# Per-head norms, rotary turns and gates computed inside the projections that feed them, and expert outputs written as plain rows

## The reference

```python
# first block, even layer: gated linear attention, its output gated by silu(r)
o = o * lax.rsqrt(jnp.mean(o * o, axis=-1, keepdims=True) + EPS)
o = (o * g_gla * jax.nn.silu(r))
# first block, odd layer: attention, 8 query heads, 2 key/value heads of 128
q = rms_norm((h @ w_q).reshape(B_, L, ATT_HEADS, HEAD_DIM), g_q)   # then apply_rope(q, cos, sin)
k, v = ...                                                          # k: rms_norm, then apply_rope on the latents
def apply_rope(t, cos, sin):
    t1, t2 = jnp.split(t, 2, axis=-1)
    return jnp.concatenate([t1 * cos - t2 * sin, t1 * sin + t2 * cos], axis=-1)
s = jnp.einsum('bkgqd,bksd->bkgqs', q, k) * (HEAD_DIM ** -0.5)      # softmax over s, times v
# second block: HGRN2 gates, forward and backward, from columns q, f_fw, f_bw, i, g of h @ w_in
logf = jnp.log(lbd + (1.0 - lbd) * jax.nn.sigmoid(fr))
kf = (1.0 - lbd) * jax.nn.sigmoid(-fr)          # cumulative sums of logf, exponentials, chunked scan
o = o * lax.rsqrt(mean(o * o) + EPS) * norm_g * jax.nn.silu(g)
# second block: mixture of 64 experts, each of 512 tokens goes to 8
y = _swiglu(h[tok], wg[e], wu[e], wd[e]) * gw[:, None]
out = out.at[tok].add(y)                        # sum over a token's 8 experts, plus a shared expert
```

## Time and profile before

| | |
|---|---|
| time, median of 3 runs | 4281.18 us (4280.32 to 4283.61) |
| the profiled execution's own time | 4279.15 us |
| its span in the profile | 4277.3 us |
| busy: PE, PEld | 3600.4 us (84%), 2155.2 us (50%) |
| busy: DVE, ACT, POOL | 1260.6 us (29%), 832.1 us (19%), 338.0 us (8%) |
| HBM read, written | 454.25 MB, 37.22 MB |
| granted PE clock, mean | 0.907 |

### The profile page before, as it was taken

The page is one execution under the profiler, slowest core; times in us unless marked ns, Lnnn a source line. Parts: engine busy times, 40 slices in busy tenths (PEclk is TensorE's granted clock), DMA queues, the critical chain, the costliest instruction groups (busy, mean ns, idle before and its releaser), DMA issues. The chain is left out here.

```text
span 4277.3 us, 63533 instructions
## 1 busy us (share of the span) xinstructions
PE 3600.4 (84%) x26072; PEld 2155.2 (50%) x26072; DVE 1260.6 (29%) x2655; ACT 832.1 (19%) x1497; POOL 338.0 (8%) x439
## 2 busy tenths in 40 slices
PE   4698568999999977999998948996956879999975
PEld 1255354555555535644443528993525445555543
DVE  0000352222210126322204584444026232222222
ACT  0010331211100113321101052332033212222211
POOL 2000000000000000000001000000000024343332
PEclk7799778999999987999998959997977889999997
DMA  9911001111111100022211000000100369999996
GB/s 385 388 45 41 3 25 40 45 54 50 45 54 46 58 16 25 25 79 79 76 68 68 30 9 3 4 4 33 54 15 27 117 220 342 344 347 347 341 366 221
DMA packets 97371, 485.34 MB, mean 113 GB/s; under 512 B 14912, under 2 KB 19552, under 8 KB 66320
## 3 DMA queue, kind: packets, MB, share of 16 engines
q1 hardware_dynamic: 74352, 435.21, 27.1%
q0 software_dynamic: 22816, 47.14, 4.8%
HBM read 454.25 MB, written 37.22 MB: 115 GB/s over the span
## 5 line engine op out<-in xcount | busy, mean ns | idle before, releaser
L438 PE MATMUL psum<-arena 128*128 128x512 f32 x2112 | 1018.7, 599 | 52.5 <-PEq L1048 29.6
L536 PE MATMUL psum<-arena 128*128 128x512 f32 x1408 | 663.8, 593 | 4.2 <-ACT arena L376 4.2
L438 PEld LDWEIGHTS psum<-arena 128*128 128x128 f32 x2112 | 402.6, 191 | 322.8 <-issue 278.6
L2700 PE MATMUL psum<-arena 128*64 128x256 f32 x3072 | 357.6, 380 | 41.5 <-DMA arena<-exp_w_in 41.3
L440 PEld LDWEIGHTS psum<-arena 128*128 128x128 f32 x1168 | 221.8, 190 | 283.6 <-issue 283.6
L536 PEld LDWEIGHTS psum<-arena 128*128 128x128 f32 x1408 | 266.3, 189 | 194.1 <-issue 172.8
L440 PE MATMUL psum<-arena 128*128 128x256 f32 x1168 | 349.2, 379 | 0.0
L2700 PEld LDWEIGHTS psum<-arena 128*64 128x64 f32 x3072 | 222.0, 135 | 206.5 <-DMA arena<-exp_w_in 60.1
L564 DVE SCALAR_TENSOR_TENSOR arena<-psum,arena 128x511 f32<-128x511 f32 (+1 forms) x132 | 83.2, 658 | 552.2 <-ACT arena L548 552.2
L538 PEld LDWEIGHTS psum<-arena 128*128 128x128 f32 x704 | 133.1, 189 | 169.6 <-issue 169.6
L538 PE MATMUL psum<-arena 128*128 128x256 f32 x704 | 209.7, 378 | 0.0
(11 more groups left out here) (460 smaller groups left out, 4277.1 us busy)
## 6 DMA issues: line engine op xcount, KB each, us to landing
arena<-exp_w_in SPq DMA_DIRECT2D x207, 1024.0 KB
arena<-w_mod_r_in SPq DMA_DIRECT2D x18, 4096.0 KB
arena<-w_ffn_up_in SPq DMA_DIRECT2D x88, 512.0 KB, 3.3
arena<-w_ffn_down_in SPq DMA_DIRECT2D x16, 1408.0 KB, 5.9
arena<-w_in_in SPq DMA_DIRECT2D x35, 512.0 KB, 3.2
arena<-w_even_in_in SPq DMA_DIRECT2D x17, 512.0 KB, 3.3
arena<-w_qkv_in SPq DMA_DIRECT2D x12, 512.0 KB, 3.2
arena<-acc SPq DMA_DIRECT2D x12, 512.0 KB, 8.1
```

The lines of the kernel that those rows point to most:

```text
L438: mm = pe.matmul(ps[:, 2 * b, :], lhsT, src[:, k, 0:LAT], start=(k == 0), stop=(k == kt - 1))
L536: mm = pe.matmul(ps[:, 2 * b, :], lhsT, A[:, k, 0:LAT], start=(k == 0), stop=(k == KD - 1))
L2700: mm = pe.matmul(ps[64 * c:64 * c + 64, 0, 0:256], xt[u][:, k, :], wgu[w][:, k, :, c * P:(c + 1) * P], start=(k == 0), stop=(k == KD - 1))
```

## The change

- `project("qkv")` and `qk_norm_rope` become one stage, `qkv_in`. The weights are rolled, so that the keys come first, then the values, then the queries; the list `QKV_JOBS` orders 12 tiles, two jobs `kn` and two `vt` over three pairs of PSUM banks. ACT squares each tile from PSUM, PE sums the squares over the channels as one column per 128 tokens (44 small matmuls), DVE turns the raw tile from PSUM with three products with the gain (two of them of half height, reading one half of the partitions and writing the other) and a sum. The keys' roots are spread to rows by 12 matmuls with the identity and multiplied in (`kn`); the queries' roots are not multiplied in but handed to attention as a scale per row (`rq`). The permutation and the reciprocals of whole tiles go.
- `project("hgp")` and `hgrn_gates` become `hgrn_in`: the f tiles come first, ACT takes the sigmoids, Silus and copies from PSUM as tiles finish, with the logarithms of one direction after tiles 3 and 7 and the exponentials after tiles 5 and 10; DVE's sums and products run beside them. The copy by POOL becomes a DMA on SP in `hgrn_scan`.
- The gates' Silu in `head_norm` goes: `project("evi")` and `hgrn_in` apply it on the way out of PSUM.
- Experts: each (token, expert) pair has its own row in `yrows` (16 half rows of 2 KB per token). The scatter writes without adding and skips empty slots by a bounds check. The zeroing goes. The routing table has a third value per (token, expert), the pair's rank within the token, made by 4 scans on DVE. At the end SP reads 32 KB per token in four DMAs of 4 MB into two buffers, and the shared expert's 2 MB; DVE folds 8 rows to 4 and 4 to 2, and PE sums the rest with the shared part while it transposes (24 matmuls for each of the four).

The diff, cut to its core:

```diff
-        project(nc, m, "evi", evi, m["A"], [T] * 17, copy_out(m, big, [T] * 17), norm=Norm(m, T, 0, (0, 0)))
+        project(nc, m, "evi", evi, m["A"], [T] * 17, copy_out(m, big, [T] * 17, range(8, 12)), norm=Norm(m, T, 0, (0, 0)))
...
-        sizes = [LAT] * 8 + [T] * 4
-        project(nc, m, "qkv", qkv, m["A"], sizes, copy_out(m, big, sizes), norm=Norm(m, T, 2, (1, 0)))
-        qk_norm_rope(nc, m, io)
+        qkv_in(nc, m, io, qkv, Norm(m, T, 2, (1, 0)))
...
-        sizes = [LAT] * 4 + [T] * 12 + [LAT] * 4
-        project(nc, m, "hgp", hgp, m["A"], sizes, copy_out(m, big, sizes), norm=Norm(m, T, 4, (2, 0), kept=True))
-        hgrn_gates(nc, m, io)
+        hgrn_in(nc, m, hgp, Norm(m, T, 4, (2, 0), kept=True))
...
+        return "act", lambda act, s, b: act.activation(dst[:, t, 0:sizes[t]], pair_banks(m["ps"], b, sizes[t]),
+                                                       ACT.Silu if t in silu else ACT.Copy)
...
-                act.activation(r[:, h, 0:n], r[:, h, 0:n], ACT.Silu).then_inc(s["sr"], 1)
...
+QKV_JOBS = [("k", 0), ("k", 1), ("v", 0), ("v", 1), ("q", 0), ("kn", 0), ("q", 1), ("kn", 1), ("q", 2), ("vt", 0), ("q", 3),
+            ("vt", 1), ("q", 4), ("q", 5), ("q", 6), ("q", 7)]
...
+def qkv_in(nc, m, io, feed, norm):
...
+    released = {"k": ("rope", 0), "q": ("rope", 2), "kn": ("kn", 0), "v": ("vc", 0), "vt": ("vo", 0)}
...
+            def sums(kind, i):
+                n = turned(kind, i)
+                if n == 0:
+                    pe.wait_ge(s["nxn"], KD)
+                pe.wait_ge(s["sq"], n + 1)
+                for t in range(width(kind) // P):
+                    o = ps[:, 6, i * TT + t:i * TT + t + 1] if kind == "k" else ps[:, 7, 4 * i + t:4 * i + t + 1]
+                    mm = pe.matmul(o, sq[:, n % 2, t * P:(t + 1) * P], m["ones"][:, 0:1], start=True, stop=True)
+                mm.then_inc(s["sm"], 1)
+
+            norm.pe(pe, s)
+            f, before = 0, None
+            for j, (kind, i) in enumerate(QKV_JOBS):
+                b = j % 3
+                if j >= 3:
+                    was, w = QKV_JOBS[j - 3]
+                    sem, base = released[was]
+                    pe.wait_ge(s[sem], base + w + 1)
+                if kind == "kn":
+                    pe.wait_ge(s["kr"], 1)
+                    for t in range(TT):
+                        c = i * TT + t
+                        mm = pe.matmul(ps[:, 2 * b + t // 4, t % 4 * P:(t % 4 + 1) * P],
+                                       kroot[:, c:c + 1].to_broadcast([P, P]), m["ident"], start=True, stop=True)
+                    mm.then_inc(s["wide"], 1)
+                elif kind == "vt":
+                    pe.wait_ge(s["vc"], i + 1)
+                    for t in range(TT):
+                        mm = pe.transpose(ps[:, 2 * b + t // 4, t % 4 * P:(t % 4 + 1) * P], dst[:, 10 + i, t * P:(t + 1) * P],
+                                          m["ident"])
+                    mm.then_inc(s["vt"], 1)
+                else:
+                    feed.arrived(pe, f)
+                    for k in range(KD):
+                        if f == 0:
+                            pe.wait_ge(s["na"], k + 1)
+                        lhsT = feed.tile(m, f)[:, k, :]
+                        mm = pe.matmul(ps[:, 2 * b, :], lhsT, m["A"][:, k, 0:LAT], start=(k == 0), stop=(k == KD - 1))
+                        if kind != "q":
+                            mm = pe.matmul(ps[:, 2 * b + 1, 0:CTX], lhsT, m["A"][:, k, LAT:T], start=(k == 0), stop=(k == KD - 1))
+                    mm.then_inc(s["mm"], 1)
+                    f += 1
+                    if before is not None:
+                        sums(*before)
+                    before = (kind, i) if kind != "v" else None
+            sums(*before)
...
+                if kind in "kq":
+                    n, w = turned(kind, i), width(kind)
+                    if n >= 2:
+                        act.wait_ge(s["sm"], n - 1)
+                    act.activation(sq[:, n % 2, 0:w], pair_banks(ps, b, w), ACT.Square).then_inc(s["sq"], 1)
...
+                    if i == 1:
+                        act.wait_ge(s["sm"], 2)
+                        act.activation(kroot, ps[:, 6, 0:12], ACT.Sqrt, scale=1.0 / P, bias=m["misc"][:, 0:1]
+                                       ).then_inc(s["krt"], 1)
...
+                    p, x, t = ps[:, 2 * b, :], dst[:, h, 0:LAT], t1[:, n % 2, :]
+                    g = cols[:, COL["gqk"] + h:COL["gqk"] + h + 1]
+                    dve.wait_ge(s["sq"], n + 1)
+                    if n >= 2:
+                        dve.wait_ge(s["fin"], n - 1)
+                    dve.scalar_tensor_tensor(x, p, g, cos, MUL, MUL)
+                    dve.scalar_tensor_tensor(t[lo, :], p[hi, :], g[hi, :], sin[hi, :], MUL, MUL)
+                    last = dve.scalar_tensor_tensor(t[hi, :], p[lo, :], g[lo, :], sin[lo, :], MUL, MUL)
+                    if kind == "k":
+                        last = dve.tensor_scalar(dst[:, h, LAT:T], ps[:, 2 * b + 1, 0:CTX], g, None, MUL)
+                    last.then_inc(s["rope"], 1)
+                    dve.wait_ge(s["rope"], n + 1)
+                    dve.tensor_tensor(x, x, t, ADD).then_inc(s["fin"], 1)
+                if (kind, i) == ("k", 1):
+                    dve.wait_ge(s["krt"], 1)
+                    dve.reciprocal(kroot, kroot).then_inc(s["kr"], 1)
+                if kind == "kn":
+                    x = dst[:, 8 + i, :]
+                    dve.wait_ge(s["wide"], i + 1)
+                    dve.wait_ge(s["fin"], i + 1)
+                    dve.tensor_tensor(x, x, pair_banks(ps, b, T), MUL).then_inc(s["kn"], 1)
+            dve.wait_ge(s["qrt"], 1)
+            own.link(dve.reciprocal(qroot, qroot))
+            dve.tensor_scalar(rq[:, 0, :], qroot, scale, None, MUL)
+            dve.tensor_scalar(rq[:, 1, :], qroot, -scale, None, MUL)
...
-                dve.tensor_scalar(x[:, 0:1], x[:, 2:3], -scale, None, MUL).then_inc(s["nm"], 1)
+                dve.tensor_tensor(x[:, 0:1], x[:, 2:3], rq[:, 1, g:g + 1], MUL).then_inc(s["nm"], 1)
...
+def hgrn_in(nc, m, feed, norm):
...
+    sizes = [T] * 8 + [LAT] * 4 + [T] * 4 + [LAT] * 4
...
-            pool.tensor_copy(m["A"][:, 0:4, 0:LAT], at(HG_Y, 4, T)[:, :, 0:LAT])
...
+            def logs(d):
+                act.wait_ge(s["act"], 4 * d + 4)
+                for n in range(4 * d, 4 * d + 4):
+                    act.activation(cum[:, n, :], cum[:, n, :], ACT.Ln, scale=lb1[:, n:n + 1], bias=lb[:, n:n + 1]
+                                   ).then_inc(s["ln"], 1)
+
+            def decays(d):
+                for n in range(4 * d, 4 * d + 4):
+                    act.wait_ge(s["mid"], n + 1)
+                    act.activation(q_hat(n), cum[:, n, 0:LAT], ACT.Exp).then_inc(s["ep"], 1)
+                    act.wait_ge(s["ep"], n + 1)
+                    act.activation(cum[:, n, :], cum[:, n, :], ACT.Exp, scale=-1.0).then_inc(s["en"], 1)
+
+            norm.act(act, s)
...
+            for t in range(N):
+                x = pair_banks(ps, t % 4, sizes[t])
+                act.wait_ge(s["mm"], t + 1)
+                if t < 8:
+                    act.activation(cum[:, t, :], x, ACT.Sigmoid)
+                    out = act.activation(f[:, t, :], x, ACT.Sigmoid, scale=-1.0)
+                elif t < 12:
+                    out = act.activation(q[:, t - 8, :], x, ACT.Silu)
+                elif t < 16:
+                    out = act.activation(v[:, t - 12, :], x, ACT.Copy)
+                else:
+                    out = act.activation(g[:, t - 16, :], x, ACT.Silu)
+                out.then_inc(s["act"], 1)
+                if t in (3, 7):
+                    logs(t // 4)
+                if t in (5, 10):
+                    decays(t // 8)
...
+            def sums(d):
+                for n in range(4 * d, 4 * d + 4):
+                    dve.wait_ge(s["ln"], n + 1)
+                    running_sum(dve, m["rst64"], cum[:, n, :], cum[:, n, :], d).then_inc(s["cu"], 1)
+                    if n % 4:
+                        centre(n - 1)
+                centre(4 * d + 3)
+
+            def keys(d):
+                for n in range(4 * d, 4 * d + 4):
+                    dve.wait_ge(s["en"], n + 1)
+                    dve.scalar_tensor_tensor(f[:, n, :], f[:, n, :], lb1[:, n:n + 1], cum[:, n, :], MUL, MUL)
+
+            def queries(d):
+                for n in range(4 * d, 4 * d + 4):
+                    dve.wait_ge(s["act"], 9 + n % 4)
+                    dve.wait_ge(s["ep"], n + 1)
+                    dve.scalar_tensor_tensor(q_hat(n), q[:, n % 4, :], 64.0 ** -0.5, q_hat(n), MUL, MUL)
+
+            sums(0)
+            keys(0)
+            sums(1)
...
+            queries(0)
+            keys(1)
+            queries(1)
...
+            sp.dma_start(m["A"][:, 0:4, 0:LAT], at(HG_Y, 4, LAT)).then_inc(s["y"], 16)
+            sp.wait_ge(s["y"], 16)
...
-            sp.wait_ge(s["z"], 1)
-            sp.dma_start(acc[LAT:ROWS, :], zero).then_inc(s["st"], 16)
```

(36 more changed lines are left out.)

277 lines of the change are left out of this document (118 added, 159 removed).

## The result

| | median us | runs | ratio to before, 95% |
|---|---|---|---|
| before | 4282.40 (4280.32 to 4285.74) | 4 | 1 |
| changed | 4140.22 (4138.39 to 4143.31) | 4 | 0.9671 [0.9658, 0.9683] |

A forecast was written before the change was run, and what follows sets the result against it. PE was taken to bound the projections, DMA the expert loop with PE's floor close under. Terms -82.5 - 59.5 - 58 - 1 + 41.6 = -159.4 on 4279.15 gave 4119.8; with 2.0 for the median, 4122 us, range 4100 to 4155.

The forecast's parts named there:

- queries and keys: Qkv stage: norms and turns move into the projection, attention starting 110.3 us after the first tile instead of 194.8; -82.5 us.
- HGRN's gates: HGRN's projection: the 59.87 us gate stage goes, its work hidden beside PE's tiles; -59.5 us.
- loop, 80 subs: Expert loop, first part: DMA falls to 513 us, PE becomes the bound, 553 us in all; -34 us.
- loop, 15 subs: Expert loop, second part: 122.8 us of DMA, less about 5 for a full ring, 118 us; -24 us.
- end of the experts: After the expert loop: reading back and summing the rows takes 65.1 us instead of 23.45; +41.6 us.
- PE's floor of 6.88 us per sub: Expert loop: two subs start 6.88 us apart where nothing waits for weights, 550 us for 80 subs.
- the two equations: Expert loop: both parts' gather and scatter times solved for DMA prices, 6.2 us per MB adding scatter, 2.2 gather.
- Rival (b): Expert loop: a plain scatter costs as much per MB as an adding one, only empty slots saved; 4137 us, chance 0.19.
- ring full, worth about 5 us: Expert loop, second part: it starts with the weights' ring full, taking about 5 us off 122.8.
- The chain: End of the experts: loads, DVE and PE in sequence, quarter 3's load waiting for quarter 1's buffer; 65.1 us.
- (c): Merged projections: ACT or DVE come late, 20 us in all; 4141 us, chance 0.10.
- (a): Whole kernel: all terms come out as summed, 4122 us; chance 0.46.

The follow-up runs named there:

- add_full: The changed kernel with the old expert rows and end, the adding scatter skipping its empty slots: 4129.29 us, ratio 0.9637.
- Four_buffers: The changed kernel with four buffers instead of two for the rows read back, so the fourth load waits for nothing: 4131.29 us, ratio 0.9648.
- four_folds: Four_buffers with the last two steps of each quarter's sum on DVE, PE only transposing: 4128.03 us, ratio 0.9644.
- norms_undone: The changed kernel with the old query and key projection, norm stage and attention scale: 4212.44 us, ratio 0.9843.
- sums_twice: The changed kernel with each of the 44 column sums made twice: 135.81 us from the norm's table load to attention, 11.8 more, one execution.

## Why the prediction was right, and where it was off

| term | predicted | in the profiled execution |
|---|---|---|
| queries and keys | -82.5 | 194.8 to 115.3: -79.5 |
| HGRN's gates | -59.5 | 241.6 to 184.2: -57.4 |
| Silu, router | 0 | -0.5, -0.4 |
| loop, 80 subs | -34 | 586.9 to 554.1: -32.8 |
| loop, 15 subs | -24 | 141.7 to 124.6: -17.2 |
| from the last sub to the first read | -1 | 10.2 to 7.7: -2.5 |
| end of the experts | +41.6 | 23.45 to 69.58: +46.1 |
| all else | 0 | +8.4 |
| sum | -159.4 | -135.8 |

**Queries and keys.** The mechanism held: no gaps in PE, DVE and ACT hidden, one barrier. What was mis-sized is the price of the small matmuls. I took one transpose's 0.137 us for each of them. A float32 matmul is two instructions in these traces, though, and only a transpose is one. 44 sums came to 9.9 us instead of 6.0 and the twelve spreading matmuls to 2.8 instead of 1.7. The row that would have told stood in the same view of before as the one I used: attention's 192 matmuls of the transposes' shape (busy us, mean ns).

```profile
L1232 PE MATMUL psum<-arena 128*128 128x128 f32 x384 | 47.9, 274 | 0.0
```

Hence 0.25 us for a matmul and 0.137 for a transpose. The first tile took 12.1 us where I let it come down to 10.35 (1.8 us). ACT's norm is hidden beneath it, as I said, but PE itself runs its first 4.33 us at a granted clock of 0.61, which in before lay under the norm's pace and which I had left out. And the way from the last big matmul to attention 5.3 against 4.1 + 1.1 + 0.5 of sums. I had set 2 us aside for bubbles; there were none.

**HGRN's gates.** As summed, 2 us short: the first tile again, 1.7 us above its pace, with a granted clock of 0.65 in its first 4.3 us. The tail, Silu, load, exponential and barrier, took 3.3 us from 3091.29, as it was built up. Of ten table loads nine fell beside PE's tiles; the tenth, 1.28 us, is the one in this tail.

**The loop's first part** came to 554.1 us against 553 forecast, but partly for a wrong reason. PE's floor of 6.88 us per sub was the right bound. DMA, however, was to be free for 40 of 553 us and is at 0.98: the weights took 449.9 instead of 440.7 us and the software queue 93.1 instead of 72. The step at fault is the two equations. They gave 6.2 us per MB for adding and 2.2 for a gather; the runs give 4.3 and 3.5 for a MB more (of empty rows, and of gathers of one row), and a plain write of empty rows 2.1, less than the 2.61 I took from the output's writes. Two equations with two unknowns can be solved exactly even when what they leave out (packets without bytes, a cost per row) is not small. Rival (b), that a plain scatter costs as much as an adding one and only the empty slots are saved, is refuted by add_full, which saves just them: 15.2 us in the loop where the changed kernel saves 49.3. Its own sum was off too: it put the first part at PE's floor, 550, while its prices give 440.7 + 33.1 + 93.2 = 567 us of DMA, and add_full took 577.65.

**The second part** missed by 6.6 us. The failing step is the "ring full, worth about 5 us": the queues' time came to 112.5 + 11.2 = 123.7 us and the part took 124.6, with nothing taken off. That no reserve of weights had been built up, DMA being full in the first part too, is the likely reason; no run here isolates it. The rest is traffic: gathers and scatters took 0.090 x 124.57 = 11.2 us instead of 8.7.

**The end.** The chain was the right one, down to the fourth load behind PE: 65.1 us predicted, 69.6 measured. The landings of quarters 0 and 1 were right within 0.4 us (12.1, 27.0). PE's quarter was mis-sized at 5.9 us, and it stands twice in the chain, with 8.2 and 8.1 us, which is the whole miss: again 24 matmuls were priced by a transpose (0.246), while they are 48 instructions at 0.17. Four_buffers takes out the first of these links and four_folds shortens the second, and they gain 6.9 and 4.9 us in the stretch.

**All else** was assumed to stay. It came to +8.4 us: 4.9 before the qkv stage, where the code hardly differs, 4.9 between attention and RWKV's output stage, 2 to 6 of which recur with every merged qkv stage, and -1.4 for the rest. The 4.9 ahead of the qkv stage are scatter between kernels: by PE's own records the modulations are 4.1 us longer than in before and the first feed-forward stage 2.5, the GLA scan 2.8 shorter, while the other kernels, with the same code there, have 192.2 to 195.7 us for the modulations and either 461.8 or 464.3 for the feed-forward stage. The profiled execution was also the slowest of its four.

Of the signs that the prediction named, attention came at 115 instead of 110 us, the scan at 184 instead of 182, the loop's steps mostly at 6.88 us; DMA's share in the first part is just below 1, the last 15 subs took 124.6 instead of 118, and the end 69.6 instead of 65. The error is of one sign: every large term was taken too well, by 1 to 7 us. The number itself, 4140, lies nearer to rivals (b) with 4137 and (c) with 4141 than to (a), but by neither's way: add_full answers (b), and (c), a late ACT or DVE in the merged projections, does not fit PE's 111.96 of 115.33 and 180.82 of 184.20 us busy. It is (a) with its errors added up.

## What to carry to other kernels

Count a small operation in instructions, from a row of the same kind (a float32 matmul and a transpose of the same shape differ by two), before putting it between big ones: on a full engine each is paid in full. When a saving frees one resource at a stage where two are near their floor, read the other's floor first, and look at what the change adds at the stage's end: here 50 us won in the loop came back as 46 of reading and summing, and 21 of those were to be had by buffers, by order and by dividing the sum. Try the cheaper half of a change by itself: the old adding scatter with its empty slots skipped was 11 us faster than the changed kernel, because it kept the short end. An adding scatter can be twice as dear as a plain one, and skipping empty rows brought nothing where PE had become the bound.

## What the runs showed of the hardware

- An indirect scatter that adds costs 4.3 us of DMA time for a MB more of empty rows, a plain one 2.1; its issue on POOL takes 1.57 us against 1.02; and behind the last one POOL waits 3.6 us with all slots added, 2.2 with all written, and 1.6 with full slots only, added or plain.
- Stages of identical code differ from kernel to kernel, and the granted clock with them. The GLA scan, which no kernel here touches, took 122.5 us (from its own table load to that of the head norm) at a granted clock of 0.71 in before, 119.7 at 0.73 in the changed kernel and 114.6 at 0.77 in norms_undone. Windows of before and of norms_undone:

```profile
502.00:623.40 121.40, 77.53 (x406) 68.41 (x406) 58.15 (x186) 38.05 (x110) 0.00 (x0) 0.71 0.01 3
```

```profile
507.00:621.30 114.30, 69.89 (x409) 61.18 (x408) 58.21 (x186) 38.77 (x111) 0.00 (x0) 0.77 0.01 3
```

  PE is busy 61 to 64% of the time there, in small pieces. Differences of a few us in a whole run are for this reason no evidence of a part; the stage's own length is.
- A run of big matmuls need not keep the clock up if one-column matmuls break into it (sums_twice, 0.64 with PE busy throughout); that they are the cause rests on one execution.
- Two dozen matmuls of the end took 5.59 us at a granted clock of 1.00 (the third quarter in four_buffers, 1.7 us behind the second); that kernel's other quarters took 7.0 to 8.1 us at 0.79 to 0.68, and the changed kernel's 7.2 to 8.2.
- The first tile of both merged projections runs its first 4.3 us at a granted clock of 0.61 and 0.65, behind 2.5 us in which PE stood idle in the qkv stage, and is 1.7 to 1.8 us longer for it than the tiles behind it.
